# Two streams one behind the other at the norms between dense stages

## The reference

```
h  = rms_norm(x, g_pre) * (1 + scale) + shift          # norm, then a dense stage
z  = h @ w_in            (2048 x 4608), attention and gMLP on z give o (2048 wide)
x  = x + gate * rms_norm(o @ w_out, g_post)             # w_out 2048 x 2048
h  = rms_norm(x, g_pre2) * (1 + scale2) + shift2
f  = (silu(h @ w_gate) * (h @ w_up)) @ w_down           # 5632 wide
x  = x + gate2 * rms_norm(f, g_post2)
```

## Time and profile before

| | us |
|---|---|
| median of 3 runs (2479.89 to 2483.84) | 2479.94 |
| the profiled execution | 2478.37 |
| its span, first to last instruction | 2476.6 |
| PE busy | 2332.2 (94%) |
| DVE busy | 1475.0 (60%) |
| ACT busy | 984.9 (40%) |
| POOL busy | 66.2 (3%) |
| mean DMA rate | 246 GB/s |

### The profile page before, as it was taken

How to read it: one execution, slowest core, us unless ns; L and a number is a source line. 1 busy time by engine, 2 the same in 40 slices (tenths; PEclk the granted TensorE clock), 3 DMA queues, 4 the chain that set the end, 5 groups by cost and what they waited for, 6 DMA issues and landing times.

```text
span 2476.6 us, 28164 instructions
## 1 busy us (share of the span) xinstructions
PE 2332.2 (94%) x10892; PEld 1816.5 (73%) x10892; DVE 1475.0 (60%) x1583; ACT 984.9 (40%) x1253; POOL 66.2 (3%) x90
## 2 busy tenths in 40 slices
PE   5999978989999999999979998798999999999997
PEld 1467745768888887888757776475888888878886
DVE  2244454568886788688765444545788644554455
ACT  2233343454444443334444333344444444434443
POOL 1001020000000000000000101000000000000000
PEclk8999989989999999999989999998999999999999
DMA  9978778758877887687756877776777666656664
GB/s 338 354 253 286 253 286 298 270 205 264 270 252 248 269 266 253 225 277 262 269 179 212 280 277 233 282 279 214 256 266 261 219 195 188 189 184 192 191 220 137
DMA packets 269318, 609.94 MB, mean 246 GB/s; under 512 B 19116, under 2 KB 19296, under 8 KB 267840
## 3 DMA queue, kind: packets, MB, share of 16 engines
q1 hardware_dynamic: 264832, 589.37, 71.3%
q0 software_dynamic: 4352, 18.76, 2.0%
HBM read 603.79 MB, written 5.45 MB: 246 GB/s over the span
## 4 chain that ended last, share of the span: by engine, by line
PE 86%; DMA 5%; issue 4%; DVE 2%; ACT 2%; POOL 0%; SPq 0%; POOLq 0%; DVEq 0%; ACTq 0%
PE bank_A L727 40%; PE bank_B L727 38%; DMA mraw<-in_mod_w 5%; PE bank_M L783 3%; PE bank_X L811 2%; PE bank_M L772 1%; PE bank_T L803 1%; ACT junk L1039 0%; PE bank_M L717 0%; DVE wlo L1256 0%; DVE x L1405 0%; DVE f L1331 0%; PE bank_A L897 0%; ACT prob L1127 0%; DMA edge<-in_c_edge 0%
## 5 line engine op out<-in xcount | busy, mean ns | idle before, releaser
L1256 DVE TENSOR_TENSOR wlo<-raw,whi 128x1024 fp32r<-128x1024 f32 x736 | 899.3, 1224 | 818.0 <-ACT whi L1025 817.7
L1025 ACT CAST whi<-raw 128x1024 fp32r<-128x1024 f32 x736 | 770.7, 1049 | 1215.4 <-PE bank_A L727 604.1
L727 PE MATMUL bank_A<-whi,xt_lo 128*128 128x512 f32 x1152 | 455.6, 396 | 3.2 <-DVE xt_lo L1310 3.2
L727 PE MATMUL bank_A<-wlo,xt_hi 128*128 128x512 f32 x1152 | 451.9, 392 | 0.0
L727 PE MATMUL bank_A<-whi,xt_hi 128*128 128x512 f32 x1152 | 451.3, 392 | 0.0
L727 PE MATMUL bank_B<-whi,xt_lo 128*128 128x512 f32 x1088 | 428.1, 393 | 0.0
L727 PE MATMUL bank_B<-wlo,xt_hi 128*128 128x512 f32 x1088 | 424.8, 390 | 0.0
L727 PE MATMUL bank_B<-whi,xt_hi 128*128 128x512 f32 x1088 | 424.3, 390 | 0.0
L1278 DVE SCALAR_TENSOR_TENSOR acc<-mraw,cond,acc 128x1024 f32<-128x1024 f32 x240 | 297.0, 1279 | 0.0
L727 PEld LDWEIGHTS bank_A<-whi,xt_lo 128*128 128x128 f32 x1152 | 218.4, 190 | 67.6 <-issue 22.8
L727 PEld LDWEIGHTS bank_A<-whi,xt_hi 128*128 128x128 f32 x1152 | 218.3, 189 | 46.2
(11 more groups left out here) (186 smaller groups left out, 1414.4 us busy)
## 6 DMA issues: line engine op xcount, KB each, us to landing
mraw<-in_mod_w SPq DMA_DIRECT2D x384, 512.0 KB, 5.4
raw<-in_w_gate SPq DMA_DIRECT2D x176, 512.0 KB, 4.1
raw<-in_w_up SPq DMA_DIRECT2D x176, 512.0 KB, 4.2
raw<-in_w_down SPq DMA_DIRECT2D x176, 512.0 KB, 4.5
raw<-in_w_in SPq DMA_DIRECT2D x144, 512.0 KB, 5.6
raw<-in_w_out SPq DMA_DIRECT2D x64, 512.0 KB, 5.5
gate_mix<-gate_rows POOLq DMA_DIRECT2D x4, 1024.0 KB, 6.3
gate_ffn<-gate_rows POOLq DMA_DIRECT2D x4, 1024.0 KB, 9.0
```

Source lines behind the costliest of these rows:

```text
L727: mm = pe.matmul(bank[f"{pair}{s}"][:], xs[:, k, t], ws_[:, slot, kb, :], start=(k == 0 and n == 0), stop=(k == nk - 1 and n == 2))
L1025: act.copy(whi[:, ph % RING], raw[:, ph % RING]).then_inc(hi_ready, 1)
L1256: dve.tensor_tensor(wlo[:, ph % RING], raw[:, ph % RING], whi[:, ph % RING].bitcast(F32), ALU.subtract).then_inc(lo_ready, 1)
```

## The change

At each norm between dense stages, and at the end, the last four pieces of the stage before are used by stream 0 alone, then by stream 1; at the norms the first four pieces of the stage behind are used in the same manner (`APART` = 4). PE's last product of stream 0 raises a new semaphore, `half_done`, and stream 0's norm starts there. So `w_used` for these pieces rises only in stream 1's pass. DVE, ACT and POOL get a new order, `turnover`, with four inverse roots of one stream each in place of two of both streams (two at the end); four pieces instead of two are split inside it. Blocks of columns are turned in the order of `turn_order`: two of stream 0, two of stream 1, then alternately; PE turns blocks 2 and 3 only after stream 0's pass over the first four pieces, 4 and 5 within stream 1's pass, 6 and 7 in the fifth and sixth piece. ACT scales blocks 1, 2, 3, 5 and 7, DVE 0, 4 and 6. The last pair of blocks is worked behind the splits of the next stage's fifth and sixth piece (`second`).

In the output stage the modulation pieces are spread: five bursts of half a chunk, after pieces 4, 9, 14, 20 and 25 of 32, and only the last half chunk stays behind the last unit. SP's order follows (`OUT_FETCH`). At the end x is stored stream by stream. The start of the kernel only changes the form of its calls.

```diff
-LEFT = 2
...
+APART = 4
+
+
+def turn_order(l, which):
+
+    if l == which == 0:
+        return [(s, b) for b in range(ND) for s in range(2)]
+    return [(0, 0), (0, 1), (1, 0), (1, 1), (0, 2), (1, 2), (0, 3), (1, 3)]
+
+
+def scaled_by_act(l, which, i):
+
+    return i % 2 == 1 or (l + which > 0 and i == 2)
+
+
+def edge_of(l, which):
+
+    return 2 * l + which
+
+
+OUT_MODS = {3: (0, range(0, 4)), 8: (0, range(4, 8)), 13: (1, range(0, 4)), 19: (1, range(4, 8)), 24: (2, range(0, 4))}
+OUT_FETCH = {4: (0, (0, 1)), 5: (0, (2, 3)), 11: (0, (4, 5)), 12: (0, (6, 7)), 16: (1, (0, 1)), 17: (1, (2, 3)),
+             22: (1, (4, 5)), 23: (1, (6, 7)), 27: (2, (0, 1)), 28: (2, (2, 3)), 31: (2, (4, 5, 6, 7))}
...
+                for q in range(LEAD, ND * UNIT):
+                    i, j = divmod(q, UNIT)
+                    both(u + i, w, i * CH, js=[j])
+                    if q in OUT_FETCH:
+                        mi, js = OUT_FETCH[q]
+                        mod_chunk(m + mi, l, js)
...
+            for s in range(2):
+                for n in range(ND):
                     c = slice(n * CH, (n + 1) * CH)
-                    sp.wait_ge(x_new, 16 * DEPTH - 8 + 2 * n + s + 1)
+                    sp.wait_ge(x_new, 16 * DEPTH - 8 + ND * s + n + 1)
...
+                    for s in range(2):
+                        power(ms[:, s:s + 1], rstd[:, s:s + 1], ms_ready, k + s + 1, rstd_ready)
+                    return
+                for s in (0, 0, 1, 1):
+                    k += 1
+                    power(ms[:, s:s + 1], rstd[:, s:s + 1], ms_ready, k, rstd_ready)
...
+                n = nk // KB
+                for js in (range(first), range(first, n - last), range(n - last, n)):
+                    together = js.start == first and js.stop == n - last
+                    for streams in [(0, 1)] if together else [(0,), (1,)]:
+                        for j in js:
+                            if streams[0] == 0:
+                                pe.wait_ge(lo_ready, u * UNIT + (ph + j + 1))
+                            slot = (ph + j) % RING
+                            for kb in range(KB):
+                                k = j * KB + kb
+                                if ready:
+                                    ready(k, streams)
+                                mm = products(pair, k, hi, lo, slot, kb, nk, streams=streams)
+                            if streams[-1] == 0:
+                                if j == n - 1:
+                                    mm.then_inc(half_done, 1)
+                                continue
+                            mm.then_inc(w_used, 1)
+                            if j in behind:
+                                mod(m, behind[j])
+                            dve_vector(u * UNIT + ph + j)
...
+                def ready(k, streams):
+                    if streams == (1,) and k == 0:
+                        turn_x(l, which, 2)
+                        turn_x(l, which, 3)
+                    elif streams == (1,) and k in (2, 5):
+                        turn_x(l, which, 4 + k // 5)
+                    elif k in (9, 11):
+                        turn_x(l, which, 6 + k // 11)
                     if k % 4 == 0:
-                        pe.wait_ge(xt_ready, xt_count(l, which) - 8 + 2 * (k // 4 + 1))
+                        pe.wait_ge(xt_ready, done + {(0,): 1 + k // 4, (1,): 3 + k // 4, (0, 1): 2 + k // 2}[streams])
...
+                def x_squares(s):
+                    for n in range(ND):
+                        act.wait_ge(x_new, 8 * edge_of(l, which) + ND * s + n + 1)
+                        square(x[:, s, n * CH:(n + 1) * CH], ssx[:, s, n:n + 1])
+
+                n = ND - 1
+                if which == 0:
+                    act.wait_ge(half_done, edge_of(l, which) + 1)
+                    act.copy(f[:, 0, n * CH:D], bank["B0"][:]).then_inc(freed["B0"], 1)
+                act.wait_ge(freed["B0"], use["B0"] + 3)
+                f_square(0, n)
+                if last_edge(l, which):
+                    act.wait_ge(freed["B1"], use["B1"] + 3)
+                    return f_square(1, n)
+                split(u, ph + pieces)
+                split(u, ph + pieces + 1)
+                x_squares(0)
+                act.wait_ge(freed["B1"], use["B1"] + 3)
+                f_square(1, n)
+                if m:
+                    mod_row(m)
+                split(u, ph + pieces + 2)
+                split(u, ph + pieces + 3)
+                x_squares(1)
+                l, which = l + which, 1 - which
                 act.wait_ge(vec_ready, vec_count(l, which))
-                for b in range(ND):
-                    pre_part(l, which, b)
+                pre_high(l, which, 0)
+                pre_scale(l, which, 1)
+                pre_high(l, which, 1)
+                pre_scale(l, which, 2)
+                pre_high(l, which, 2)
+                pre_scale(l, which, 3)
+                pre_high(l, which, 3)
+                pre_pair(l, which, 4)
...
+                def last_chunk(s):
+                    if which == s == 0:
+                        return
+                    if s == 0:
+                        dve.wait_ge(half_done, now + 1)
+                    else:
+                        dve.wait_ge(w_used, u * UNIT + ph + pieces)
+                    b = f"B{s}"
+                    if which:
+                        dve.tensor_tensor(f[:, s, c], f[:, s, c], bank[b][:], ALU.add).then_inc(freed[b], 1)
+                    else:
+                        dve.tensor_copy(f[:, s, c], bank[b][:]).then_inc(freed[b], 1)
+
+                def add(s):
+                    for n in range(ND):
+                        t = slice(n * CH, (n + 1) * CH)
+                        dve.scalar_tensor_tensor(out=x[:, s, t], in0=f[:, s, t], scalar=rstd[:, s:s + 1], in1=x[:, s, t],
+                                                 op0=ALU.mult, op1=ALU.add).then_inc(x_new, 1)
+
+                last_chunk(0)
+                gated(l, which, ND - 1, 0, sq + 7)
+                mean_square(ssq, sq + 7, slice(0, 1))
+                if not end:
+                    split(u, ph + pieces)
+                dve.wait_ge(rstd_ready, rs + 1)
+                add(0)
+                last_chunk(1)
+                if end:
+                    gated(l, which, ND - 1, 1, sq + 8)
+                    mean_square(ssq, sq + 8, slice(1, 2))
+                    dve.wait_ge(rstd_ready, rs + 2)
+                    return add(1)
+                split(u, ph + pieces + 1)
+                mean_square(ssx, sq + 11, slice(0, 1))
+                gated(l, which, ND - 1, 1, sq + 12)
+                l2, w2 = l + which, 1 - which
+                dve.wait_ge(rstd_ready, rs + 2)
+                mean_square(ssq, sq + 12, slice(1, 2))
+                normal(l2, w2, 0, 1)
+                dve.wait_ge(rstd_ready, rs + 3)
+                add(1)
+                if vectors:
+                    vectors()
+                dve.wait_ge(vec_ready, vec_count(l2, w2))
+                pre_scale(l2, w2, 0)
+                mean_square(ssx, sq + 16, slice(1, 2))
+                pre_low(l2, w2, 0)
+                split(u, ph + pieces + 2)
+                dve.wait_ge(rstd_ready, rs + 4)
+                normal(l2, w2, 2, 3)
+                pre_low(l2, w2, 1)
+                split(u, ph + pieces + 3)
+                pre_low(l2, w2, 2)
+                normal(l2, w2, 4, 5)
+                pre_low(l2, w2, 3)
+                normal(l2, w2, 6, 7)
+                pre_pair(l2, w2, 4)
...
+                    ahead(split, i * 2 + u, second=None if i else lambda: pre_pair(l, 0, 6))
+                for i in range(ND):
+                    at = {q % UNIT: mj for q, mj in OUT_MODS.items() if q // UNIT == i}
+
+                    def burst(k, streams):
+                        if k % KB == 0 and k // KB - 1 in at:
+                            mi, js = at[k // KB - 1]
+                            mod(m + mi, js)
+                    dense(i + u, "AB"[i % 2], i // 2 + use["AB"[i % 2] + "0"], xt_hi, xt_lo, ready=burst,
+                          last=APART if i == ND - 1 else 0)
...
```

More of the change, by code:

```diff
@@ L931, in pair @@
                 def pair(i, ready=None):
-                    dense(i * 2 + u, "A", i + use["A0"], xt_hi, xt_lo, ready=ready, m=i + m, behind=IN_FIRST)
+                    dense(i * 2 + u, "A", i + use["A0"], xt_hi, xt_lo, ready=ready, m=i + m, behind=IN_FIRST,
+                          first=APART if ready else 0)
                     dense(i * 2 + (u + 1), "B", i + use["B0"], xt_hi, xt_lo, m=i + m, behind=IN_SECOND)
@@ L988, in _, with ahead @@
                         dense(u, p, use2[p + "0"] + i // 2, ht_hi, ht_lo, nk=4 * n, ph=2 * n * i,
-                              ready=hidden_ready if i else hidden_first)
-        def ahead(split, u, ph=0, pieces=UNIT, between=None, leave=0):
+                              ready=hidden_ready if i else hidden_first,
```

(29 more changed lines are left out.)

251 lines of the change are left out of this document (109 added, 142 removed).

## The result

| | before | after |
|---|---|---|
| median (20 runs each) | 2479.91 | 2493.64 |
| ratio | | 1.0047, 95% 1.0036 to 1.0059 |
| profiled execution | 2478.37 | 2497.18 |
| its span | 2476.6 | 2495.4 |
| PE busy | 2332.2 | 2344.7 |

The change makes the kernel slower by 0.47%, 11.7 us. A later comparison gave 1.0052 (1.0037 to 1.0067). The forecast was 1.9 us faster. Executions of one kernel spread over some 20 us (2471.9 to 2493.6 before, 2481.4 to 2500.2 after), so a profile tells where time goes, and the ratios tell how much.

The account below looks back on a forecast made before the run. PE was busy 94%, its norm gaps set by a serial DVE, ACT and POOL chain. +1.7 - 3.2 + 0.4 - 2.65 = -3.75, plus one clock fall +1.9, gave -1.9: 2478.0 us, range 2469 to 2487.

Parts of the forecast that it names:

- norm 1: First norm: cost 28.1 us including a fifth modulation burst, against 26.4 before, so +1.7.
- norm 2: Second norm: cost 23.7 us against 26.9 before, so -3.2.
- norm 3: Third norm: cost 28.1 us including a fifth modulation burst, against 27.7 before, so +0.4.
- falls in short waits: PE's nine short waits, three a norm: the clock falls in one, +1.9 us; bounds none or all nine, 17.
- the chain: DVE, ACT and POOL steps at each norm: PE restarts 12.5 or 11.7 us after stage end, not 19.8.
- DMA would not be late in the output stage: Output stage: closer modulation bursts cost nothing; a rival with 1 us for each of ten gave 2486, chance 0.06.
- rows 8: Profile rows cited for the clock: one rest of 3.0 us in which it fell, one in which it did not.
- Rival (b): Clock falls in two waits of every norm, six falls: +7.7 us, 2487.6; chance 0.14.
- all nine waits: Short waits at the norms: by the skill's rule every one would count, time about 2493.
- the fifth burst: Output stage: one more burst of modulation products, 1.85 us, which before lay inside the norm.
- the gain at the end: Kernel end: x complete 7.1 us after PE's last product instead of 9.8, -2.65; -1.7 with a slower root.
- has a serial tail with little ahead of it: Late turns of blocks in the norms: scaling, rounding and splitting behind them make PE wait 2.3, 2.9 and 3.6 us.

Follow-up runs that it names:

- k_short_2: The changed kernel with 5, 6 and 7 filler products in each norm's three short waits, timed again beside the unaltered changed kernel: ratio to before 1.0014.
- k_short: The changed kernel with 5, 6 and 7 filler products in the three short waits of every norm, first timing: ratio to before 1.0026.
- a_first0: The changed kernel, but the first four pieces behind a norm take both streams together again: ratio to before 1.0039.
- a_last0: The changed kernel, but the last four pieces ahead of a norm and of the end take both streams together again: ratio to before 1.0146.
- b_fill_and_end: The kernel before with fillers in its norms' long gaps and the two streams apart at the very end: ratio to before 0.9951.
- after_timed: The changed kernel again, unaltered, timed beside its version with fillers in the short waits: ratio to before 1.0052.

## Why the prediction was wrong

In its own reckoning (from the end of the last product, less 21.8, with a fifth burst of 1.9 at the first and third norm):

| | before | forecast | measured |
|---|---|---|---|
| norm 1 | 26.4 | 28.1 | 34.5 |
| norm 2 | 26.9 | 23.7 | 27.4 |
| norm 3 | 27.7 | 28.1 | 32.8 |
| falls in short waits | | one, +1.9 | seven (in the rows above) |
| end: x complete behind PE | 9.8 | 7.1 | 6.5 |

**Right: the chain.** Restart 12.3, 11.6 and 12.2 us behind the stage's end (12.5, 11.7, 12.5 forecast), stream 0's pass over at 19.8 (19.9), three waits of 2.5, 2.8 and 3.4 (2.3, 2.9, 3.6), the burst that fills the middle one at the second norm to 0.9 (1.0). With the falls taken away by fillers, norms 1 and 3 cost what the forecast gives them: 48.5 and 48.3, where 28.1 less the burst plus 21.8 makes 48.1, and k_short_2 gives 49.2 and 49.3. That DMA would not be late in the output stage was right too: PE waited for `mraw` at most 0.7 us in one of the two output stages and not at all in the other.

**Wrong: the count of falls.** The failed step is "I take one, +1.9, near the lower end, because these waits stand between dense runs". Measured are six or seven. At the first norm the whole excess over the forecast is in three stretches: 1.5 us between the starts of stream 1's pass and piece 5, 2.8 in pieces 5 and 6, 1.9 in pieces 7 and 8, each with the clock at 0.50 at its head. The three norms together are 12.9 us over a forecast that has one fall in it, so seven cost 14.8, 2.1 each, if all of it is theirs: 1.9 was a fair price, and only the long spell of 6.0 us cost 2.8. The reason given did not hold. Both rests of rows 8 stand in attention, the one in which the clock held too, so neither tells of a dense surrounding; and the one in which it fell was 3.6 us long, from 1539.66 to 1543.23, of which the row is a cut. Even by these two rows, nine waits at one chance in two are four or five falls, not one. The trace of before has seven rests of 2.5 to 3.6 us that begin at full clock, and in or just behind four of them it fell. One of the seven stands between products of a dense stage, and the clock fell 1.3 us behind its end (the wait in PE's timeline, then the stretch behind it, granted clock 0.51):

```profile
1213.74 1.21 PE L811 MATMUL bank_X<-ident,hid 128*128 128x128 f32 x8 [2.77 <-issue]
...
1215.00:1218.50 3.50, 3.50 (x10) 2.74 (x9) 2.51 (x3) 1.51 (x2) 0.00 (x0) 0.51 1.01 417
```

This wait of 2.8 us is in all 16 profiles of this study, and in 13 of them the clock fell. Rival (b) named the place and the mechanism with six falls and 2487.6, and had a chance of 0.14.

The Trainium skill, "TensorE: Matmul & The Clock Gate", section "HAM oscillation — how this bites in real kernels", tells of a kernel in which every burst behind a wait of some 3 to 5 us started at the throttled clock. The prediction carried that over to all nine waits, though it had six of them at 2.9 us or less, and got about 2493. The runs show 20 falls in 27 waits, all where the wait was over 2.4 us. That the measured median is 2493.6 is in part luck: nine falls at 1.9 are 17.1 us, the seven measured came to 14.8 at most, and the output stages were 2.4 dearer.

Timed, the falls are a smaller part. With no fall the forecast is 0.9985; k_short and k_short_2, in which the clock holds, stand at 1.0026 and 1.0014, 7 to 10 us above it (the intervals reach 3 us either way). The traces place 2.4 us of that in the output stages and up to 2 in the overfilled wait; the rest is not placed.

**Too small: the fifth burst.** 1.9 a layer was forecast. The output stages grew by 3.0 and 3.3 us, and the modulation moved alone cost 5.2 us (2.0 to 8.4). Of the growth 0.7 and 1.2 us are in the first six products, at the clock that attention left behind; without them it is 2.3 and 2.1.

**Too small: the gain at the end**, 3.3 instead of 2.65. The root took 0.5, not 0.7, and DVE took stream 1's chunk 0.6 behind PE.

The sum in the profile: norms and bursts +13.7, the rest of the two stages +2.4, the end -3.3, and 12.8 beside a timed 11.7. The profiled executions differ by 18.8: attention of the second layer was 4.6 us faster in the profile of before than after, and the stages between the first norm and the second 1.3. The first stretch takes 276 to 281 us in all other profiles and 272 only there, so it is not of the change.

**Not seen: that the waits were a matter of order.** The forecast said that each late turn "has a serial tail with little ahead of it", and took the order as given. That was the larger sum: the fillers in the short waits take 12 us off the three norms, and the early turns 27 more.

## What to carry to other kernels

When a change cuts one long wait into several short ones, price each as wait plus restart at half clock until a run shows otherwise; here, in five profiles (the changed kernel three times, a_first0, a_last0), the clock fell in 14 of 15 waits of 3.4 us and in 11 of 12 of 2.5, and in none of 0.9 or less. Where PE itself issues the first step of a chain that it later waits for, look how long its helpers stand idle before that step: idle time on DVE and ACT that ends with PE's turn (6.7 and 6.9 us here) was the sign that the step is issued too late, and it could be moved ahead without PE waiting for its input. A wait that keeps its length when the work ahead of it comes 5 us later was such a latency here, not load.

## What the runs showed of the hardware

Products that nobody reads, put in PE's waits, hold the granted clock at 1.00 (2.4 GHz): 31 fillers over 13.5 us at a norm of the kernel before, and the products behind them at 0.227 us. In the kernel before they alone are worth 0.25% (0.12 to 0.37). In that run the clock held behind two waits of 2.4 us for `xtmp` and fell behind the third, which is otherwise the same; in b_fill_and_end it fell behind all three. The same wait of the same kernel goes either way: at 2.5 us of the first norm the clock fell in two profiles of the changed kernel and held in after_timed. One wait of 3.4 us, the third norm's in a_last0, did not make it fall. The spells at half clock behind a short wait of the changed kernel ended 3 to 4 us or 5 to 6 us behind the first product; no run shows what sets which.
